# Index queries projected in three rounded passes, after the index keys, in a one-layer streaming encoder step

## The chip, the cores and the metric

The kernel runs as one program on one core of a Trainium2 chip. The metric is device time in microseconds (us). Before the change three runs gave a median of 1030.94 us (1030.78 to 1036.11).

The core has five engines that run side by side and meet only at semaphores: PE (matrix multiplies and transposes, with results in PSUM, the accumulator memory), DVE (vector work), ACT (activations and copies), POOL (a slower vector engine that also issues some transfers) and SP (which here only issues DMA transfers). On-chip data lie in SBUF.

## The reference, cut to what matters

One layer of an encoder is computed for 512 prompt tokens and 32 sample tokens, 1024 features each: a normalised input `h`, one wide projection of it, window attention, sparse attention, a merge, then a mixture of experts and an embedding gate. The change is in the part that picks keys for the sparse attention:

```python
qa, ka, va, qb, kb, vb, iq, ik, iw, ga, gb = jnp.split(jnp.dot(h, w_in), IN_SPLITS, axis=-1)
...
dots = jnp.einsum('bqhd,bsd->bqhs', iq, ik) * IDX_SCALE
score = jnp.einsum('bqh,bqhs->bqs', iw * IDX_HEAD_SCALE, jax.nn.relu(dots))
_, sel = lax.top_k(score, topk)
```

`iq` are the index queries (8 heads of 64, so 512 columns of `w_in`), `ik` the index keys (64 columns), `iw` 8 weights. A separate small table `rel_bias` gives a bias by the distance of query and key.

## The kernel before, in words

Every engine has one list of instructions, in the order in which the code writes them; nothing reorders them. Two tables only number the PSUM buffers: `WIDE` (three slots of two banks) and `NARROW` (two slots of one bank). Each says, for a use, which slot it gets and which earlier use must have been read out first, and by which engine.

The 544 tokens are in five tiles (four of 128, one of 32). The 1024 features are eight planes of 128. The steps of the front, in PE's order:

1. Transposes of the five normalised tiles (L900). DVE reads them out and multiplies by the gain (L1856): that is `hT`, the input with features on the partitions.
2. The bias table: one product of 32 buckets by 384 distances (L905). DVE reads it out, changes it in two small steps (L1875 to L1878) and signals `tabp_ready`. SP waits for this signal before it issues the write of the table, 128 times repeated, to memory outside the core (`toeplitz`, 3 MB). POOL waits for the same signal (L745) before it starts on its own list.
3. The index queries: four groups `m` of 128 columns, in each eight planes by two halves of 272 tokens, in plain f32 (`project`, L881).
4. The index keys and weights `ikw`: for each token tile eight products with 72 columns, in plain f32 (L888).
5. The keys turned: the prompt's (L920), then the cached ones and the sample's (L925, L926).
6. `dots`: 24 products for the prompt and 2 groups for the sample, each over a high and a low part of the keys (L940, L936). ACT applies the relu (L1522), DVE adds up the scores (L1914, L1917) and later picks the best eight at a time (L1933, L1937).
7. Keys and values of the sparse branch (`kvb`), then of the window branch (`kva`), in three passes each (L952), with their transposes; then the queries `qb` and `qa`, in three passes (L980). Then attention begins (L1014).

Three passes means this: a value `v` is split into a rounded high part (type fp32r, made by ACT, L1490) and the rounded remainder (made by DVE or POOL, L743, L758). Then high by high, high by low and low by high are added up in PSUM. `hT_f` and `hT_lo` are the two parts of `hT` for all 544 tokens. For step 7 they are made while steps 3 and 4 run.

After each index query group ACT stores a rounded high part (L1503) and DVE the remainder (L1886); after the turned keys the same two (L1507, L1900).

`slab[0]` is the SBUF place of the index query weights, and then of the `qb` weights; `slab_ikw` that of the key weights, and then of the `kva` weights. SP issues the `qb` load once the last index query group is in PSUM, and the `kva` load once the prompt's keys are turned. Both come behind the `toeplitz` write in SP's list and in its DMA queue.

On ACT the list after the last relu is: wait for the `kva` weights, make their high part (the `high` helper, L1490), then read out the five `kvb` tiles (L1532), each of which frees a `NARROW` slot.

Of the kernel before, what the change touches and what calls it, by code (L numbers as in the profile page):

```python
# [23 lines left out]
F32 = mybir.dt.float32  # L24
# [8 lines left out]
P = 128  # L33
# [43 lines left out]
CONSTS = 6  # L77
# [44 lines left out]
def ring(uses, slots):  # L122
# [16 lines left out]
    [(('xT', t), 'dve') for t in range(TILES)] + [(('iq', m), 'dve') for m in range(4)]  # L139
    + [(('ikT', s), 'dve') for s in 'ps']  # L140
# [4 lines left out]
    [('table', 'dve')] + [(('ikw', t), 'dve') for t in range(TILES)]  # L145
# [79 lines left out]
def _program(nc, A, ctx):  # L225
# [26 lines left out]
    def sem(name):  # L252
        return ctx.enter_context(nc.semaphore(name))
# [25 lines left out]
    for lo, hi in ((0, 16), (16, 24), (24, 32), (32.5, 40.5), (40.5, 48.5), (48.5, 56.5), (68.5, 73), (80, 97), (97.25, 114.25)):  # L279
        twin(arena, "front", int(lo * 256), int(hi * 256))  # L280
# [34 lines left out]
    hT_lo = at(114.25, [KD, NT])  # L315
    score = hb[:, 0:3 * (PAST + NS)].rearrange("p (b n) -> p b n", b=3)
# [157 lines left out]
    consts_in, gains_in = sem("consts_in"), sem("gains_in")  # L474
# [64 lines left out]
    def _(sp):  # L539
# [7 lines left out]
        for n, g in enumerate(['g_attn', 'g_ffn', 'g_ple']):  # L547
            load(gains[:, n, :], A[g][0].rearrange("(p c) -> p c", c=KD), gains_in)
# [19 lines left out]
        load(sink_in[:, :], A['attn_sink'].to_broadcast([P, HEADS]), consts_in)  # L568

# [146 lines left out]
    def _(pool):  # L716
# [28 lines left out]
        pool.wait_ge(tabp_ready, 1)  # L745
# [3 lines left out]
        pool.wait_ge(sw_high, 1)  # L749
# [10 lines left out]
        pool.wait_ge(sw_high, 2)  # L760
# [8 lines left out]
        query_weights_low(3, slab[0], qb)  # L769
# [13 lines left out]
        query_weights_low(7, slab[1], qx)  # L783
# [84 lines left out]
    def _(pe):  # L868
# [26 lines left out]
        for t in range(TILES):  # L895
# [7 lines left out]
        pe.wait_ge(table_in, 32)  # L903
        open_slot(NARROW, 'table', narrow_out)
        pe.matmul(ps[0:16, 6, 0:DIST], relb[0:BUCKETS, :], onehot[0:BUCKETS, :], start=True, stop=True)\  # L905
            .then_inc(narrow_full, 1)

        pe.wait_ge(slab_in['iq'], 16)
        pe.wait_ge(wide_out['dve'], WIDE[('xT', 4)].out)
        for m in range(4):  # L910
            slot = open_slot(WIDE, ('iq', m), wide_out)
            project(slot, lambda c: slab[0][:, c, m * P:(m + 1) * P], P, None, 0).then_inc(wide_full, 1)
        pe.wait_ge(slab_in['ikw'], 16)
        for t in range(TILES):
            slot = open_slot(NARROW, ('ikw', t), narrow_out)
            by_token(ps[:, 6 + slot, :], slab_ikw, IKW, t).then_inc(narrow_full, 1)
        w = wide(open_slot(WIDE, ('ikT', 'p'), wide_out))
# [3 lines left out]
        mm.then_inc(wide_full, 1)  # L921
        w = wide(open_slot(WIDE, ('ikT', 's'), wide_out))
# [23 lines left out]
        for br, s, c_k, kv_n in (('b', slab_kvb, cb_k, kv_b), ('a', slab_kva, None, kv_a)):  # L946
            pe.wait_ge(sw_split, 'ba'.index(br) + 1)
# [24 lines left out]
        for n, (q, s, dst) in enumerate((('qb', slab[0], qb), ('qa', slab[1], qx))):  # L972
            for m in range(4):
                w = wide(open_slot(WIDE, (q, m), wide_out))
                pe.wait_ge(sw_split, 3 + 4 * n + m)
# [494 lines left out]
    def _(act):  # L1470
# [10 lines left out]
        for t in range(TILES):  # L1481
            act.wait_ge(x_in[t], 16)
            r = ROWS[t]
            act.activation(xf[0:r, t, :], x_nat[0:r, t, :], ACT.Square, accum_out=nrm[0:r, t:t + 1]).then_inc(squares, 1)
# [14 lines left out]
        for m in range(4):  # L1499
# [5 lines left out]
        for i, (part, lo, cols) in enumerate((('p', 0, NP), ('s', NP, PAST + NS))):  # L1505
            w = wide(close(WIDE, ('ikT', part), wide_full))
            act.activation(rounded(ik_hi[:, lo:lo + cols], "front"), w[:, 0:cols], ACT.Copy).then_inc(ik_high, 1)  # L1507

# [311 lines left out]
    def _(dve):  # L1820
# [48 lines left out]
        dve.wait_ge(gains_in, 48)  # L1869
# [3 lines left out]
        dve.wait_ge(consts_ready, 1)  # L1873
        close(NARROW, 'table', narrow_full)
        dve.tensor_copy(tab[0:16, :], ps[0:16, 6, 0:DIST]).then_inc(narrow_out['dve'], 1)  # L1875
        dve.wait_ge(narrow_out['dve'], NARROW['table'].out)
        link(dve.tensor_tensor(nrm[0:16, 31:32], tab[0:16, 0:1], nrm[0:16, 30:31], ALU.mult))
        dve.tensor_scalar(tab[0:16, :], tab[0:16, :], nrm[0:16, 31:32], -1.0, ALU.subtract, ALU.mult).then_inc(tabp_ready, 1)  # L1878
        dve.memset(msk, 0.0)

        for m in range(4):
# [8 lines left out]
        for t in range(TILES):  # L1890
            r = ROWS[t]
            slot = close(NARROW, ('ikw', t), narrow_full)
            src = ps[0:r, 6 + slot, :]
            dve.tensor_copy(ik_n[0:r, t, :].rearrange("p (a n) -> p a n", a=2),
                            src[:, 0:HD].unsqueeze(1).to_broadcast([r, 2, HD]))
            dve.tensor_scalar(iw_n[0:r, t, :], src[:, HD:IKW], IW_SCALE, None, ALU.mult).then_inc(narrow_out['dve'], 1)
        for i, (part, lo, cols) in enumerate((('p', 0, NP), ('s', NP, PAST + NS))):
# [3 lines left out]
                              rounded(ik_hi[:, lo:lo + cols], "front").bitcast(F32), ALU.subtract).then_inc(wide_out['dve'], 1)  # L1901

# [537 lines left out]
```

## Time and profile before

| what | value |
|---|---|
| three runs | 1030.94 us median (1030.78 to 1036.11) |
| the profiled execution, its own time | 1036.8 us |
| its span, first to last instruction | 1035.0 us |
| TensorE clock granted over the span (mean) | 0.967 of full speed |
| PE busy | 925.9 us (89% of the span) |
| DVE, ACT, POOL busy | 378.2, 256.5, 132.4 us |
| chain that ended last: PE, DMA, DVE, ACT | 63%, 29%, 4%, 2% |

A time in the trace is counted from the first instruction. A group of the profile names engine, source line, output and input, and how often it runs. A plain f32 matmul appears as two records, so 64 of them read x128. The front described above is the stretch from 0 to 162 us; attention, merge and routing follow, and then the expert weights are streamed.

### The profile page before, as it was taken

The numbers are of one execution on the slowest core, as the hardware profiler recorded it, in microseconds if no ns is written. First come the engines' busy times: TensorE is split into PE (matmuls) and PEld (weight loads), VectorE is DVE, ScalarE is ACT, GpSimd is POOL, SyncE is SP. The second block draws the span as 40 slices with busy tenths as digits, with TensorE's granted clock in tenths as the row PEclk, the third lists the DMA queues.
The fourth block names the chain that finished last, engine by engine and source line by source line (L and its number), as shares of the span: only waits on it lengthen the run. The fifth ranks groups of instructions, "written<-read, shape, count | busy, mean of one in ns | idle before, by whom it ended". The sixth has DMA issues, their size and how long they took to land.

```text
span 1035.0 us, 14155 instructions
## 1 busy us (share of the span) xinstructions
PE 925.9 (89%) x5699; PEld 591.2 (57%) x5702; DVE 378.2 (37%) x974; ACT 256.5 (25%) x523; POOL 132.4 (13%) x136
## 2 busy tenths in 40 slices
PE   7989999999999999998999977877887888887996
PEld 7869995456999998994333322322322222234775
DVE  4179996764233436453111101101101011102796
ACT  6244326764323233221000000000000000001542
POOL 2403701113030000001111110011010110000000
PEclk9999998999999999997999999999999899999998
DMA  9850602002834316366999999999999999996601
GB/s 265 118 152 2 203 1 62 1 2 68 263 105 120 78 46 244 128 236 239 427 427 425 427 428 428 424 428 425 429 426 426 427 426 425 427 428 264 254 22 66
DMA packets 60132, 263.72 MB, mean 255 GB/s; under 512 B 11054, under 2 KB 36030, under 8 KB 46224
## 3 DMA queue, kind: packets, MB, share of 16 engines
q1 hardware_dynamic: 54160, 250.99, 63.0%
q0 software_dynamic: 5296, 9.79, 2.6%
q10 hardware_dynamic: 624, 2.23, 0.6%
q8 instruction: 36, 0.59, 0.2%
q14 instruction: 16, 0.13, 0.0%
HBM read 253.99 MB, written 16.85 MB: 262 GB/s over the span
## 4 chain that ended last, share of the span: by engine, by line
PE 63%; DMA 29%; DVE 4%; ACT 2%; issue 1%; SPq 1%; DVEq 0%; ACTq 0%
DMA arena<-in_w_up 25%; PE ps L1111 13%; PE ps L1278 12%; PE ps L980 5%; PE ps L1143 4%; PE ps L1426 4%; PE ps L1303 3%; PE ps L881 3%; PE ps L952 3%; DMA arena<-in_w_ple 2%; PE ps L1044 2%; PE ps L1014 2%; PE ps L1065 2%; PE ps L1399 1%; PE ps L1172 1%
## 5 line engine op out<-in xcount | busy, mean ns | idle before, releaser
L1278 PE MATMUL ps<-arena,hT 128*64 128x512 f32 x960 | 234.5, 641 | 39.4 <-DMA arena<-in_w_up 39.2
L1278 PEld LDWEIGHTS ps<-arena,hT 128*64 128x64 f32 x960 | 71.6, 141 | 199.3 <-issue 149.4
L2211 DVE TENSOR_TENSOR xf<-xf,ps 128x256 f32<-128x256 f32 x32 | 13.5, 421 | 401.6 <-ACT xf L1699 379.1
L1111 PE MATMUL ps<-arena_merge,arena_merge 128*128 128x256 f32 x624 | 99.7, 287 | 0.0
L1303 PE MATMUL ps<-arena,xf 128*64 128x512 f32 x336 | 76.7, 598 | 12.8 <-DVE xf L2214 12.8
L1111 PEld LDWEIGHTS ps<-arena_merge,arena_merge 128*128 128x128 f32 x624 | 87.4, 188 | 0.0
L836 POOL DMA_INDIRECT expert_rows<-xf,arena x32 | 32.2, 1007 | 425.6 <-ACT xf L1703 399.8
L1111 PE MATMUL ps<-xf_merge,arena_merge 128*128 128x256 f32 x480 | 82.0, 288 | 0.0
L1699 ACT ACTIVATE xf<-ps 128x256 f32<-128x256 f32 x30 | 11.6, 385 | 259.1 <-PE ps L1278 259.1
L1111 PEld LDWEIGHTS ps<-xf_merge,arena_merge 128*128 128x128 f32 x480 | 69.3, 188 | 0.0
L1703 ACT ACTIVATE xf<-ps 128x512 f32<-128x512 f32 x30 | 17.9, 598 | 159.8 <-PE ps L1303 159.8
L1303 PEld LDWEIGHTS ps<-arena,xf 128*64 128x64 f32 x336 | 24.3, 136 | 50.8 <-issue 43.0
L1143 PE MATMUL ps<-arena_merge,arena_merge 128*128 128x256 f32 x304 | 49.0, 286 | 1.2 <-DVE arena_merge L2045 1.0
L1303 PE MATMUL ps<-hT,xf 128*64 128x512 f32 x176 | 40.2, 598 | 6.6 <-DVE xf L2214 5.2
L1426 PE MATMUL ps<-arena_gate,hT_gate 128*128 128x512 f32 x192 | 44.4, 391 | 1.1 <-ACT arena L1741 0.6
L1143 PEld LDWEIGHTS ps<-arena_merge,arena_merge 128*128 128x128 f32 x304 | 42.9, 191 | 2.5 <-DVE arena_merge L2045 2.0
L980 PE MATMUL ps<-xf_merge,arena_front 128*128 128x272 f32 x256 | 42.9, 289 | 0.0
L2045 DVE TENSOR_TENSOR arena_merge<-arena,arena_merge 128x256 fp32r<-128x256 f32 (+2 forms) x34 | 39.9, 1228 | 5.1 <-ACT arena_merge L1490 5.0
L1490 ACT ACTIVATE arena_merge<-arena 128x256 fp32r<-128x256 f32 (+3 forms) x43 | 37.1, 919 | 16.2 <-DMA arena<-in_w_branch_a 7.2
L1426 PEld LDWEIGHTS ps<-arena_gate,hT_gate 128*128 128x128 f32 x192 | 35.8, 188 | 9.1 <-ACT arena L1741 1.0
L980 PEld LDWEIGHTS ps<-xf_merge,arena_front 128*128 128x128 f32 x256 | 36.2, 189 | 0.0
L1559 ACT ACTIVATE hT<-ps 128x256 f32<-128x256 f32 (+3 forms) x64 | 25.0, 394 | 21.9 <-PE ps L1044 21.2
(309 smaller groups left out, 1311.1 us busy)
## 6 DMA issues: line engine op xcount, KB each, us to landing
arena<-in_w_gate SPq DMA_DIRECT2D x30, 2048.0 KB, 29.4
arena<-in_w_up SPq DMA_DIRECT2D x30, 2048.0 KB, 37.0
arena<-in_w_down SPq DMA_DIRECT2D x11, 2048.0 KB, 36.4
hT<-in_w_down SPq DMA_DIRECT2D x11, 2048.0 KB, 36.5
arena<-in_w_down SPq DMA_DIRECT2D x20, 1024.0 KB, 32.2
arena<-in_w_in SPq DMA_DIRECT2D x10, 1024.0 KB, 6.2
arena<-in_w_in SPq DMA_DIRECT2D x3, 2048.0 KB, 10.5
arena<-in_w_gate SPq DMA_DIRECT2D x8, 512.0 KB, 9.0
```

Source lines behind the costliest of these rows:

```text
L836: pool.indirect_dma_start(ys, bass.IndirectOffsetOnAxis(ap=of, axis=0), src, None, bounds_check=row_bound, oob_is_err=False).then_inc(s, 16)
L881: mm = pe.matmul(w[:, a * 512:a * 512 + HALF], lhs(c), hT[:, c, a * HALF:(a + 1) * HALF], start=c == 0, stop=c == KD - 1)
L952: mm = pe.matmul(ps[0:ROWS[t], 6 + slot, 0:256], rounded(st[:, c, tok(t)]), rounded(mv[:, c, :], "front"), start=c == 0 and k == 0, stop=c ...
L980: mm = pe.matmul(w[:, a * 512:a * 512 + HALF], rounded(st, "front"), rounded(mv[:, c, a * HALF:(a + 1) * HALF]), start=c == 0 and k == 0, ...
L1111: mm = pe.matmul(w[:, 2 * lo_t:lo_t + hi_t], rounded(st[:, c, cols]), rounded(mv[:, c, lo_t:hi_t]), start=c == 0 and k == 0, stop=c == pla ...
L1143: mm = pe.matmul(w[:, q * QW:(q + 1) * QW], rounded(st[t // 2][:, t % 2, m, :]), rounded(mv[:, m, :]), start=m == 0 and k == 0, stop=m == ...
L1278: mm = pe.matmul(ps[g * BLK:(g + 1) * BLK, 2 + s, :], xsT[:, c, col:col + BLK], expert_columns(k, slice(0, 2), c, g), start=c == 0, stop=c ...
L1303: mm = pe.matmul(ps[g * BLK:(g + 1) * BLK, 6 + s, :], hidT[s][:, c % 2, c // 2 * BLK:(c // 2 + 1) * BLK], dn_at(k, c)[:, g * 512:(g + 1) * ...
L1426: mm = pe.matmul(w[:, cols], rounded(st[:, c, :], "gate"), rounded(mv[:, c, cols], "gate"), start=c == 0 and k == 0, stop=c == KD - 1 and ...
L1490: return act.activation(rounded(dst, stage), src, ACT.Copy)
L1559: act.activation(pT_sb[k2][:, j % 2, 0:tiles, j // 2 % 2, :], ps[:, 4 + u % 2, 0:tiles * P].rearrange("p (k n) -> p k n", n=P), ACT.Copy)\
L2045: return dve.tensor_tensor(rounded(v, stage), v, rounded(hi, stage).bitcast(F32), ALU.subtract)
```

## The change

`ikw` moves ahead of the index queries, and the table product behind the first index query group. The index queries are computed in three passes, as the later projections are: `hT_f` and `hT_lo` are used, and the weights are split into `iq_hi` (ACT, four groups) and a remainder in place (DVE for groups 0 and 1, POOL for 2 and 3). The turned keys are put between the groups: prompt's keys after group 0 and the table, cached and sample keys after group 1. POOL no longer waits for the table before it makes `hT_lo`. SP loads the key weights ahead of the query weights, and two of the three gain vectors with the constants.

```diff
-    [('table', 'dve')] + [(('ikw', t), 'dve') for t in range(TILES)]
+    [(('ikw', t), 'dve') for t in range(TILES)] + [('table', 'dve')]
@@ SP
+        load_gain(0, x_in[4])
+        load(slab_ikw, w_in[:, :, C_IK:C_IK + IKW], slab_in['ikw'])
+        load(slab[0], w_in[:, :, C_IQ:C_IQ + 512], slab_in['iq'])
         load(onehot[0:BUCKETS, :], A['bucket_of_distance'], table_in)
         load(relb[0:BUCKETS, :], A['rel_bias'], table_in)
-        load(slab[0], w_in[:, :, C_IQ:C_IQ + 512], slab_in['iq'])
-        load(slab_ikw, w_in[:, :, C_IK:C_IK + IKW], slab_in['ikw'])
@@ POOL
-        pool.wait_ge(tabp_ready, 1)
         for c in range(KD):
             pool.wait_ge(f_high, c + 1)
             low_of(hT_lo[:, c, :], hT[:, c, 0:NT], hT_f[:, c, :]).then_inc(f_split, 1)
+        for m in (2, 3):
+            pool.wait_ge(sw_high, m + 1)
+            low_of(slab[0][:, :, m * P:(m + 1) * P], slab[0][:, :, m * P:(m + 1) * P], iq_hi[m], "front").then_inc(sw_split, 1)
@@ PE
-        def project(slot, lhs, n_lhs, s_in, col):
-            w = wide(slot)
-            for c in range(KD):
-                for a in range(2):
-                    mm = pe.matmul(w[:, a * 512:a * 512 + HALF], lhs(c), hT[:, c, a * HALF:(a + 1) * HALF],
-                                   start=c == 0, stop=c == KD - 1)
-            return mm
+        def index_queries(m):
+            w = wide(open_slot(WIDE, ('iq', m), wide_out))
+            pe.wait_ge(sw_high, m + 1)
+            for k in range(3):
+                if k == 2:
+                    pe.wait_ge(*((iq_split, m + 1) if m < 2 else (sw_split, m - 1)))
+                for c in range(KD):
+                    if m == 0 and k < 2:
+                        pe.wait_ge((f_high, f_split)[k], c + 1)
+                    st = slab[0][:, c, m * P:(m + 1) * P] if k == 2 else iq_hi[m][:, c, :]
+                    mv = hT_lo if k == 1 else hT_f
+                    for a in range(2):
+                        mm = pe.matmul(w[:, a * 512:a * 512 + HALF], rounded(st, "front"),
+                                       rounded(mv[:, c, a * HALF:(a + 1) * HALF]),
+                                       start=c == 0 and k == 0, stop=c == KD - 1 and k == 2)
+            mm.then_inc(wide_full, 1)
@@ ACT
+        act.wait_ge(slab_in['iq'], 16)
+        for m in range(4):
+            high(iq_hi[m], slab[0][:, :, m * P:(m + 1) * P], "front").then_inc(sw_high, 1)
         act.wait_ge(slab_in['kvb'], 16)
         high(kv_hi['b'], slab_kvb, "front").then_inc(sw_high, 1)
@@ DVE
+        for m in range(2):
+            dve.wait_ge(sw_high, m + 1)
+            lo = slab[0][:, :, m * P:(m + 1) * P]
+            dve.tensor_tensor(rounded(lo, "front"), lo, rounded(iq_hi[m], "front").bitcast(F32), ALU.subtract).then_inc(iq_split, 1)
```

PE's list between the transposes of the input and the first `dots` product, before (`arena` is the SBUF area of the weights, `x_nat` here holds the index keys):

```order
L900 MATMUL ps<-ident,xf 128x32 x8
L905 MATMUL ps<-arena 16x384
L881 MATMUL ps<-hT,arena 128x272 x64
L888 MATMUL ps<-arena,hT 128x72 x32
L888 MATMUL ps<-arena,hT 32x72 x8
L920 MATMUL ps<-ident,x_nat 128x128 x4
L925 MATMUL ps<-ident,x_nat 128x128 x4
L926 MATMUL ps<-ident,x_nat 128x32
L940 MATMUL ps<-arena_front_83,arena_front_85 128x256
```

The same stretch after the change (`xf_merge_68` is `hT_f`, `arena_merge_77` is `hT_lo`; L919 is the three-pass product, L886 the keys, L927 the table, L932, L938 and L939 the turned keys); of the third and fourth group, which read like the second, only the third's first row is shown:

```order
L898 MATMUL ps<-ident,xf 128x32 x8
L886 MATMUL ps<-arena,hT 128x72 x32
L886 MATMUL ps<-arena,hT 32x72 x8
L919 MATMUL ps<-xf_merge_68,arena_front_82 128x272 x16
L919 MATMUL ps<-arena_merge_77,arena_front_82 128x272 x16
L919 MATMUL ps<-xf_merge_68,arena_front_78 128x272 x16
L927 MATMUL ps<-arena 16x384
L932 MATMUL ps<-ident,x_nat 128x128 x4
L919 MATMUL ps<-xf_merge_68,arena_front_82 128x272 x16
L919 MATMUL ps<-arena_merge_77,arena_front_82 128x272 x16
L919 MATMUL ps<-xf_merge_68,arena_front_78 128x272 x16
L938 MATMUL ps<-ident,x_nat 128x128 x4
```

The 64 plain products become 192 rounded ones; the keys come first, and their transposes no longer stand last. The last thing ahead of the `dots` is now an index query group.

DVE's list from the last readout of the transposed input on, before:

```order
L1856 TENSOR_TENSOR hT<-ps,gains 128x8x32
L1875 COPY arena<-ps 16x384
L1877 TENSOR_TENSOR nrm<-arena,nrm 16x1
L1878 TENSOR_SCALAR arena<-arena,nrm 16x384
L1879 MEMSET arena 128x912
```

And after (the five pairs of L1903 and L1905 read out the keys; the first two pairs' rows are enough here):

```order
L1882 TENSOR_TENSOR hT<-ps,gains 128x8x32
L1903 COPY x_nat<-ps 128x128
L1905 TENSOR_SCALAR x_nat<-ps 128x8
...
L1905 TENSOR_SCALAR x_nat<-ps 32x8
L1909 TENSOR_TENSOR arena_front_78<-arena,arena_front_82 128x8x128 x2
L1916 TENSOR_TENSOR arena_front_85<-ps,arena_front_85 64x544 x2
L1929 COPY arena<-ps 16x384
L1931 TENSOR_TENSOR nrm<-arena,nrm 16x1
L1932 TENSOR_SCALAR arena<-arena,nrm 16x384
```

The table's last step, behind which SP's `toeplitz` write waits, moved behind the keys' readout, two weight remainders and the first index query group.

## Rows read from the trace of the kernel before

**Rows 1.** Chain of waits, 15 to 65 us: start us, length us, what.
```profile
19.93 0.74 PE ps L905 x2
20.68 29.53 PE ps L881 x128
50.20 8.23 PE ps L888 x80
...
58.95 0.64 PE ps L920 x4
...
61.73 0.52 PE ps L940 x2
```

**Rows 2.** Timeline of PE: start us, length us, work (the last turned keys).
```profile
59.95 0.24 PE L926 MATMUL ps<-ident,x_nat 32*128 32x32 f32 x1
```

**Rows 3.** Chain of waits, 75 to 165 us.
```profile
79.63 14.31 PE ps L952 x120
...
111.99 48.51 PE ps L980 x384
...
161.15 0.63 ACT arena L1549
```

**Rows 4.** Timeline of DVE: start us, length us, work [idle before <-releaser].
```profile
21.54 0.41 DVE L1878 TENSOR_SCALAR arena<-arena,nrm 16x384 f32<-16x384 f32 x1
...
51.59 1.46 DVE L1886 TENSOR_TENSOR arena_front<-ps,arena_front 64x544 fp32r<-64x544 f32 x2 [5.88 <-ACT arena_front L1503]
...
58.67 0.14 DVE L1896 TENSOR_SCALAR x_nat<-ps 32x8 f32<-32x8 f32 x1
...
160.44 0.67 DVE L1963 TENSOR_SCALAR arena<-sink_in 32x2 f32<-32x2 f32 x4
161.84 0.06 DVE L1966 MEMSET ps<- 128x4 f32 x1 [0.73 <-ACT arena L1549]
```

**Rows 5.** Timeline of ACT.
```profile
20.56 4.49 ACT L1490 ACTIVATE xf_merge<-hT 128x544 fp32r<-128x544 f32 x8 [3.56 <-DVE hT L1856]
24.96 1.89 ACT L1490 ACTIVATE arena_front<-arena 128x2048 fp32r<-128x2048 f32 x1
...
80.21 1.91 ACT L1490 ACTIVATE arena_front<-arena 128x2048 fp32r<-128x2048 f32 x1
82.72 0.39 ACT L1532 ACTIVATE x_nat<-ps 128x256 f32<-128x256 f32 x1 [0.59 <-PE ps L952]
```

**Rows 6.** Timeline of POOL.
```profile
22.03 10.42 POOL L743 TENSOR_TENSOR arena_merge<-hT,xf_merge 128x544 fp32r<-128x544 f32 x8 [19.13 <-DVE arena L1878]
32.41 4.53 POOL L743 TENSOR_TENSOR arena_front<-arena,arena_front 128x2048 fp32r<-128x2048 f32 x1
```

**Rows 7.** Groups by line and form, DVE, whole span: count, busy us, mean ns.
```profile
L2045 DVE TENSOR_TENSOR arena_merge<-arena,arena_merge 128x1024 fp32r<-128x1024 f32 x8 | 12.1, 1512 | 0.0
```

**Rows 8.** Timeline of SP's issues.
```profile
24.90 0.43 SPq L541 DMA_DIRECT2D sink_in<-in_attn_sink  x1
25.37 0.68 SPq L541 DMA_DIRECT2D toeplitz<-arena  x1
...
50.24 9.91 SPq L541 DMA_DIRECT2D arena<-in_w_in  x2
```

**Rows 9.** DMA issues, 25.3 to 25.5, 50.2 to 50.5 and 59.3 to 60 us: KB, us to landing.
```profile
toeplitz<-arena SPq DMA_DIRECT2D x1, 3072.0 KB, 33.7
...
arena<-in_w_in SPq DMA_DIRECT2D x1, 2048.0 KB, 14.4
...
arena<-in_w_in SPq DMA_DIRECT2D x1, 1024.0 KB, 7.7
```

**Rows 10.** Stretches: length, busy us of the engines, clock, DMA share, GB/s.
```profile
54.00:56.00 2.00, 2.00 (x20) 2.00 (x20) 0.49 (x4) 0.00 (x0) 0.00 (x0) 1.00 0.91 104
60.00:62.00 2.00, 0.46 (x4) 0.35 (x4) 1.65 (x5) 0.84 (x2) 0.68 (x2) 1.00 1.05 401
62.00:66.00 4.00, 3.94 (x19) 3.71 (x19) 3.58 (x10) 2.87 (x8) 0.00 (x0) 0.59 0.96 333
```

More of the change, by code:

```diff
@@ L315, in _program @@
     hT_lo = at(114.25, [KD, NT])
+    iq_hi = [at(kb, [KD, P]) for kb in (40.5, 44.5, 52.75, 56.75)]
     score = hb[:, 0:3 * (PAST + NS)].rearrange("p (b n) -> p b n", b=3)
@@ L901, in _ @@
             mm.then_inc(wide_full, 1)
[L903 to L908, printed above, removed]
+        pe.wait_ge(slab_in['ikw'], 16)
         pe.wait_ge(wide_out['dve'], WIDE[('xT', 4)].out)
[L910 to L913, printed above, removed]
         for t in range(TILES):
@@ L916, in _ @@
             by_token(ps[:, 6 + slot, :], slab_ikw, IKW, t).then_inc(narrow_full, 1)
+        def index_queries(m):
[14 more added lines that the diff above has]
+            mm.then_inc(wide_full, 1)
+        index_queries(0)
+        pe.wait_ge(table_in, 32)
+        slot = open_slot(NARROW, 'table', narrow_out)
+        pe.matmul(ps[0:16, 6 + slot, 0:DIST], relb[0:BUCKETS, :], onehot[0:BUCKETS, :], start=True, stop=True)\
+            .then_inc(narrow_full, 1)
         w = wide(open_slot(WIDE, ('ikT', 'p'), wide_out))
@@ L946, in _ @@
         for br, s, c_k, kv_n in (('b', slab_kvb, cb_k, kv_b), ('a', slab_kva, None, kv_a)):
-            pe.wait_ge(sw_split, 'ba'.index(br) + 1)
+            pe.wait_ge(sw_split, 'ba'.index(br) + 3)
             for t in range(TILES):
@@ L1481, in _ @@
         for t in range(TILES):
-            act.wait_ge(x_in[t], 16)
+            act.wait_ge(x_in[t], 16 if t < 4 else 32)
             r = ROWS[t]
@@ L1504, in _, with index_keys @@
             ins.then_inc(q_high, 1)
-        for i, (part, lo, cols) in enumerate((('p', 0, NP), ('s', NP, PAST + NS))):
+        def index_keys(part, lo, cols):
             w = wide(close(WIDE, ('ikT', part), wide_full))
             act.activation(rounded(ik_hi[:, lo:lo + cols], "front"), w[:, 0:cols], ACT.Copy).then_inc(ik_high, 1)
+        index_queries(0)
+        index_keys('p', 0, NP)
+        index_queries(1)
+        index_keys('s', NP, PAST + NS)
+        index_queries(2)
+        index_queries(3)
         def query_weights_high(s, dst):
@@ L1868, in _, with index_queries @@
         rstd(P, 3, rstd_ready, 2)
-        dve.wait_ge(gains_in, 48)
+        dve.wait_ge(x_in[4], 32)
         for t in range(TILES):
             turned(wide(close(WIDE, ('xT', t), wide_full)), ROWS[t], t, 0).then_inc(wide_out['dve'], 1)
[L1873 to L1881, printed above, removed]
+        for t in range(TILES):
+            r = ROWS[t]
+            slot = close(NARROW, ('ikw', t), narrow_full)
+            src = ps[0:r, 6 + slot, :]
+            dve.tensor_copy(ik_n[0:r, t, :].rearrange("p (a n) -> p a n", a=2),
+                            src[:, 0:HD].unsqueeze(1).to_broadcast([r, 2, HD]))
+            dve.tensor_scalar(iw_n[0:r, t, :], src[:, HD:IKW], IW_SCALE, None, ALU.mult).then_inc(narrow_out['dve'], 1)
+        for m in range(2):
+            dve.wait_ge(sw_high, m + 1)
+            lo = slab[0][:, :, m * P:(m + 1) * P]
+            dve.tensor_tensor(rounded(lo, "front"), lo, rounded(iq_hi[m], "front").bitcast(F32), ALU.subtract).then_inc(iq_split, 1)
+        def index_queries(m):
             w = wide(close(WIDE, ('iq', m), wide_full))
@@ L1888, in _, with index_keys @@
             ins.then_inc(wide_out['dve'], 1)
[L1890 to L1897, printed above, removed]
+        def index_keys(i, part, lo, cols):
             w = wide(close(WIDE, ('ikT', part), wide_full))
@@ L1901, in _ @@
                               rounded(ik_hi[:, lo:lo + cols], "front").bitcast(F32), ALU.subtract).then_inc(wide_out['dve'], 1)
+        index_queries(0)
+        dve.wait_ge(consts_ready, 1)
+        slot = close(NARROW, 'table', narrow_full)
+        dve.tensor_copy(tab[0:16, :], ps[0:16, 6 + slot, 0:DIST]).then_inc(narrow_out['dve'], 1)
+        dve.wait_ge(narrow_out['dve'], NARROW['table'].out)
+        link(dve.tensor_tensor(nrm[0:16, 31:32], tab[0:16, 0:1], nrm[0:16, 30:31], ALU.mult))
+        dve.tensor_scalar(tab[0:16, :], tab[0:16, :], nrm[0:16, 31:32], -1.0, ALU.subtract, ALU.mult).then_inc(tabp_ready, 1)
+        index_keys(0, 'p', 0, NP)
+        index_queries(1)
+        index_keys(1, 's', NP, PAST + NS)
+        dve.memset(msk, 0.0)
+        index_queries(2)
+        index_queries(3)
         dve.wait_ge(narrow_out['dve'], NARROW_DONE['dve'])
```

33 lines of the change are left out of this document (19 added, 14 removed).

## The prediction

> **What bounds the kernel now.** I read the chain of waits first. From 20.7 to 160.5 us it is nearly all PE: the index queries take 29.53 us, the keys 8.23 us, turned keys follow, and the `dots` start at 61.73 us [rows 1]; later `kvb` (120 records in 14.31 us) and the two query projections (384 matmuls in 48.51 us) run packed [rows 3]. ACT's last readout ends at 161.78 us, and attention starts behind it. Then I read DVE's timeline at the same end: its selection and bias work is over at 160.44 + 0.67 = 161.11 us, and it then waits 0.73 us for ACT [rows 4]. So two chains run side by side from the `dots` to attention: PE's (the longer) and DVE's, 0.7 us shorter. Both start with the first `dots`. A gain ahead of the `dots` goes through only if both keep it. Behind 162 us nothing is changed, and every later load waits for progress of PE, so what attention gains in its start the end gains too.
>
> **The index queries.** Removed: 64 plain f32 matmuls, 29.53 us, 461 ns each [rows 1]. Added: 4 groups of 48 rounded matmuls of the same 272 columns. The later query projections are the same operation on the same `hT_f` and `hT_lo`: 48.51 / 384 = 126.3 ns each [rows 3]. 48 take 6.06 us, four groups 24.25 us: 5.28 us less. I take this row, since form, operands and weight changes are alike. The bounds are 120 ns (`kvb`'s 14.31 / 120 = 119 ns, at 256 columns) and 130 ns, so 23.0 to 25.0 us.
>
> The Trainium skill, "TensorE: Matmul & The Clock Gate", section "Back-to-back issue gap", gives N / 2.4 + 2.5 ns from one matmul to the next, 116 ns for 272 columns. By that the groups would be 2.0 us shorter. The trace's 126.3 ns disagrees and decides.
>
> **PE's list from 20.68 us.** The keys still wait for the last readout of `hT`. The table's 0.74 us had stood ahead of that wait, under DVE's readout; now it stands on the path.
> - keys: 20.68 + 8.23 = 28.91
> - group 0: 34.97; table: 35.71; prompt's keys (0.64): 36.35
> - group 1: 42.41; cached and sample keys (59.59 to 60.19, 0.60 [rows 1, 2], with the handover 0.7): 43.1
> - groups 2 and 3: 49.2 and 55.3.
>
> The `dots` wait until group 3 is stored. Before, the last group was in PSUM at 50.21 and DVE had stored it at 51.59 + 1.46 = 53.05 [rows 1, 4], 2.84 us. So the `dots` start at 55.3 + 2.84 + 0.05 = 58.2 us, against 61.73: 3.5 us earlier. Of the 5.28 us saved, 0.7 goes to the table and 1.3 to a longer last handover (2.9 us without PE work instead of 1.54), and the wait for the keys' readout gives 0.4 back.
>
> **What must be ready in time.** Each is hidden if earlier than PE's need.
> - High weights: ACT ends `hT_f` at 25.05 [rows 5], then four pieces of 128x1024, half of the 1.89 us for 128x2048 each, 26.0 to 29.0. Group 0 needs the first at 28.9. The query weights have landed by then (DMA traffic ahead of it is unchanged). Slack 2.9 us.
> - `hT_lo`: POOL needs 10.42 us for eight planes [rows 6] and now starts behind the first `hT_f` plane, at 21.3, so it ends at 31.7. The second pass of group 0 runs from 30.9 and needs the last plane at 32.7. Slack 1.0 us.
> - Remainder of group 0: DVE is free at 28.91 + 0.38 (its last key readout ended 0.38 us behind PE [rows 1, 4]) = 29.3 and takes 1.5 us [rows 7]: 30.8, needed at 32.9. Groups 2 and 3 on POOL: half of 4.53 us each [rows 6], so 34.0 and 36.2, needed at 47. `kvb`'s remainder ends at 40.8, needed at 76.
>
> DVE's two remainders (29.3 to 32.3) and POOL's last planes (to 31.7) run side by side, each with two inputs from SBUF, and no row of this front shows such a pair. Were both at half speed, `hT_lo` would end near 34 and PE would lose 1.3 us (rival 4). The Trainium skill, "GPSIMD Engine Reference", section "Key points", says that POOL contends with DVE instructions that read two SBUF inputs; it gives no size for it.
>
> **The table and what queues behind it.** This is the term that decides. DVE finished the table at 21.54 + 0.41 = 21.95, 1.28 us behind its matmul [rows 1, 4]. Now its copy stands behind group 0's storing: 34.97 + 2.84 = 37.81, and 1.17 us on 38.98. SP, which had been busy until 25.33 with small loads [rows 8], is idle by then and issues `toeplitz` at 39.05 instead of 25.37. It took 33.7 us to land [rows 9], at 59.07, at a steady 104 GB/s with the DMA engines 91% busy [rows 10]. `qb` was issued at 50.24 and landed 14.4 us later, at 64.64; `kva` was issued at 50.24 + 9.91 - 0.54 = 59.6 and landed at 67.3, 8.2 us behind `toeplitz` [rows 8, 9]. Until `toeplitz` ended the rate did not rise (104 GB/s at 54 to 56 us, with `qb` issued; 401 at 60 to 62 [rows 10]), so the two loads stood in a queue behind it. Afterwards `toeplitz` lands at 39.05 + 33.7 = 72.75, `qb` and `kva` (issued at 55.3 and 56) behind it, `kva` at 81.0. `qb` is wanted only near 95.
>
> Who waits for `kva`? ACT, at once behind the last relu: 80.21 before [rows 5], 76.7 now. It sits until 81.0 (4.3 us), makes the high part (1.91), and only then reads out `kvb` tile 0 (0.39): PE may start tile 2 at 83.4. PE starts `kvb` at 79.63 - 3.5 = 76.1 and has tiles 0 and 1 (2.86 us each) done at 81.8. So PE stands for 1.6 us where it stood for none. The bounds: `toeplitz` streams at once, since nothing is ahead of it now, and `kva` lands at 79.3: no stall. The loads go through one after another in their own issue-to-landing times, 72.75 + 14.4 + 7.7 = 94.8: 15.4 us of stall. I take 81.0, since the same three transfers did that in the trace. `kva`'s remainder (4.6 us on POOL, to 87.5) is in time for 94.
>
> **Nothing else.** `msk`'s memset, the key stores of POOL and the gain loads have idle engines around them.
>
> **The sum.** DVE's chain starts 3.5 us earlier and ends at 157.6. PE's chain gains 3.5 - 1.6 = 1.9 and ACT's last readout ends at 159.9: still the later one. The profiled execution would take 1036.8 - 1.9 = 1034.9 us. That one lay 5.9 us above the median of the runs, 1030.94, and the difference carries over: 1029.0 us.
>
> **Rivals.**
> 1. *`kva` is in time* (its lower bound), or the matmuls come nearer to 120 ns: the gain is 3.5 to 4.5 us, 1026.9 us. For it: in the trace `toeplitz` had other loads ahead of it. Against: the three transfers filled the queue. DVE's chain, 0.7 us shorter and started by the same `dots`, does not stand in the way.
> 2. *The queue holds ACT for long.* From a landing at 82.9 on, nothing is left of the gain (81.0 + 1.9); each us beyond is lost one to one, and above 88.1 the kernel is over 0.5% slower. At the far bound, 94.8, the loss is 15.4 - 3.5 = 11.9 us, 1042.8 us. For it: POOL's key stores now fall into the `toeplitz` write. Against: they are small, and the queue ran at 401 GB/s as soon as `toeplitz` was through.
> 3. *The clock.* After the 1.54 us without PE work around 61 us the granted clock was 0.59 on the mean from 62 to 66 us [rows 10]: of these 4 us 3.3 us were at the lower level, 1.2 GHz. It cost little, since ACT and DVE set the pace of the `dots`. Now PE stands for 2.9 us ahead of the `dots` and 1.6 us in `kvb`. If `kvb` gets such a stretch, half of it is lost, 1.6 us on PE's chain: no change, 1030.7 us.
> 4. *PE waits in group 0 for POOL's planes*: 1.3 us of the 1.9 are gone, 1030.3 us. Against: slack 1.0 us at POOL's measured pace.
>
> **How the numbers follow.** A change of under 0.5% (5.2 us) can't be told from none by measurement. Forecast 50%; rival 1, 20%; rivals 3 and 4, 20%; rival 2 beyond the zero point, 10%, of which half above 0.5%. All of the first three lie within 0.5%, but part of rival 1 together with a luckier median of the runs may pass 5.2 us. So faster 0.07, same 0.87, slower 0.06. The range runs from 1026.0 (rival 1 with 120 ns) to 1033.0 (2 us beyond no change, the near half of rival 2).
>
> **What would show it.** The first `dots` at 58.2 us; 24.2 us for 192 matmuls without gaps in group 0; `toeplitz` issued at 39.05; `kva` landing near 81; ACT idle for about 4 us on a DMA ahead of its `kva` high part; a PE gap of 1 to 2 us in `kvb`, released by ACT's readout; attention starting near 160.1. I am wrong if PE has no gap in `kvb` (then rival 1), if it is over 3.5 us (rival 2), or if the front of PE's list waits for weights or for POOL.

## The result and the profile after

| | before | after |
|---|---|---|
| median of 8 runs each | 1035.87 us (1030.78 to 1037.47) | 1040.25 us (1036.55 to 1044.47) |
| profiled execution, its own time | 1036.8 us | 1039.61 us |
| its span | 1035.0 us | 1037.9 us |
| clock granted over the span | 0.967 | 0.963 |

After / before is 1.0059, with a 95% interval of 1.0035 to 1.0082: 0.6% slower (the two medians alone stand 0.4% apart). 1029.0 us was forecast, at most 1033.0, and slower had a chance of 0.06. The eight runs of the kernel before are the three on which the forecast stood and five later ones, and those lay higher (1035.20 to 1037.47 us).

The chain of waits of the kernel after (start us, length us, what), where that of before is [rows 1, 3]:

```profile
19.68 14.05 PE ps L886 x80
33.73 7.02 PE ps L919 x48
...
42.08 6.01 PE ps L919 x48
...
48.70 12.21 PE ps L919 x96
...
60.93 0.61 ACT arena_front L1521
61.54 25.32 DMA arena<-in_w_in
...
86.89 1.91 ACT arena_front L1505
88.80 0.28 ACT x_nat L1558
```

Two lines catch the eye. The keys (L886) take 14.05 us where the same 80 records took 8.23 [rows 1]. And the chain passes through a weight load for 25.32 us: the `kva` weights.

Why the keys are slow stands in the stretches of the kernel after (length, busy us of PE, PEld, DVE, ACT and POOL with counts, clock, DMA share, GB/s; a clock of 1.00 is 2.4 GHz, 0.50 is 1.2 GHz):

```profile
18.00:20.00 2.00, 0.44 (x5) 0.35 (x5) 1.54 (x3) 0.43 (x1) 0.00 (x0) 1.00 0.87 257
20.00:22.00 2.00, 2.00 (x19) 2.00 (x19) 0.30 (x2) 2.00 (x5) 1.69 (x2) 0.94 1.10 275
22.00:24.00 2.00, 2.00 (x11) 2.00 (x11) 0.06 (x1) 2.00 (x5) 2.00 (x2) 0.50 0.81 87
...
32.00:34.00 2.00, 2.00 (x16) 1.80 (x15) 0.30 (x4) 0.00 (x0) 2.00 (x2) 0.50 0.00 0
34.00:36.00 2.00, 2.00 (x12) 2.00 (x12) 2.00 (x3) 0.00 (x0) 2.00 (x2) 0.64 0.00 0
```

PE is mostly idle from 18 to 20 us, then fully busy; at 21.8 us the clock falls to 0.50, and it comes back only at 35.4, when the wide products of group 0 have run for 1.7 us. The count of records tells the same: 19 in the 2 us that are nearly all at full clock, 11 at half. What stood in the gap before was the table's product; and in the traced execution of the kernel before, the transposes ahead of it ran at 1.2 GHz until 18.4 us and so lasted until 19.93, where here they ran at 2.4 GHz and ended near 18.1. PE's timeline of the kernel after shows the gap in brackets, and a second one in `kvb` (L967):

```profile
19.68 1.53 PE L886 MATMUL ps<-arena,hT 128*128 128x72 f32 x12 [1.56 <-DVE hT L1882]
...
89.12 0.50 PE L967 MATMUL ps<-arena_front,xf_merge 128*128 128x256 f32 x2 [1.53 <-ACT x_nat L1558]
```

The second gap was forecast, with its cause. SP's issues, and ACT's high part of `kva`, in the timelines of the kernel after:

```profile
44.83 0.68 SPq L542 DMA_DIRECT2D toeplitz<-arena  x1
60.93 10.66 SPq L542 DMA_DIRECT2D arena<-in_w_in  x2
```
```profile
86.89 1.91 ACT L1505 ACTIVATE arena_front<-arena 128x2048 fp32r<-128x2048 f32 x1 [4.51 <-DMA arena<-in_w_in]
```

The DMA issues of this kernel (KB, us from issue to landing) answer to [rows 9]:

```profile
toeplitz<-arena SPq DMA_DIRECT2D x1, 3072.0 KB, 32.6
...
arena<-in_w_in SPq DMA_DIRECT2D x1, 2048.0 KB, 22.4
...
arena<-in_w_in SPq DMA_DIRECT2D x1, 1024.0 KB, 25.3
```

`toeplitz` is issued 19.5 us later than before [rows 8], and the loads behind it land late; ACT sits 4.5 us and then reads out `kvb`'s first tile.

Two more lines matter, though their cost is hidden here. They are DVE's remainders of the query weights for groups 0 and 1 (in the view of that line: ns of the shortest, the median and the longest, and when the first and the last began), and POOL's timeline at that time:

```profile
L1909 DVE TENSOR_TENSOR arena_front<-arena,arena_front x2: 2393/4002/5611, 34.1 to 36.4; 128x1024 fp32r<-128x1024 f32 x2
```
```profile
20.31 10.43 POOL L748 TENSOR_TENSOR arena_merge<-hT,xf_merge 128x544 fp32r<-128x544 f32 x8 [17.39 <-ACT xf_merge L1505]
30.71 10.19 POOL L748 TENSOR_TENSOR arena_front<-arena,arena_front 128x1024 fp32r<-128x1024 f32 x3
```

Two instructions that were priced at 1.5 us each took 2.39 and 5.61 us. The second ended at 41.98, 1.08 us behind POOL's last remainder, that of `kvb`, which took 5.57 us and ended at 40.90.

Attention starts at 165.69 us, in DVE's timeline of the kernel after, against 161.84 [rows 4]:

```profile
165.69 0.06 DVE L2003 MEMSET ps<- 128x4 f32 x1 [2.37 <-ACT arena L1575]
```

The 3.85 us split into 2.07 at the start of the `dots` (63.80 against 61.73) and 1.78 behind it, in `kvb`. The span grew by 2.9 us, the median by 4.4. A single execution can differ that much in the later stages: from the start of attention to the end, where nothing was changed, the ten traced executions of this document took between 867.4 and 873.6 us (873.2 before, 872.2 after). In the two shortest, e2 and e3 below, the clock stayed at 1.00 from 162 to 300 us, where it was 0.96 on the mean before and after. So the start of attention, and not the total of one execution, is what the traces are compared by below.

One thing doesn't fit a simple rule on pauses. PE stood for 2.90 us ahead of the `dots` and 1.53 us in `kvb`, and the clock fell behind neither; it is at 1.00 from 52 to 110 us:

```profile
62.00:66.00 4.00, 2.10 (x13) 1.70 (x13) 3.50 (x10) 1.50 (x6) 0.00 (x0) 1.00 0.89 103
```

In the kernel before, 1.54 us were enough at the same place [rows 10].

### The profile page after: what moved, and what is told of

Same layout as the page of the kernel before. It is cut to its first block, busy times and chain, and to the rows that moved or that the text cites. A ratio compares the mean times of both kernels' runs of the same rounds, so it can differ in the third digit from the quotient of the medians.

```text
span 1037.9 us, 14298 instructions
## 1 busy us (share of the span) xinstructions
PE 928.5 (89%) x5766; PEld 593.4 (57%) x5766; DVE 386.0 (37%) x976; ACT 259.6 (25%) x527; POOL 138.0 (13%) x138
## 4 chain that ended last, share of the span: by engine, by line
PE 60%; DMA 31%; DVE 4%; ACT 2%; issue 1%; SPq 0%; DVEq 0%; ACTq 0%
DMA arena<-in_w_up 26%; PE ps L1126 13%; PE ps L1293 12%; PE ps L995 5%; PE ps L1158 4%; PE ps L1441 4%; PE ps L1318 3%; DMA arena<-in_w_in 2%; PE ps L919 2%; DMA arena<-in_w_ple 2%; PE ps L967 2%; PE ps L1059 2%; PE ps L1029 2%; PE ps L1080 2%; PE ps L886 1%
## 5 line engine op out<-in xcount | busy, mean ns | idle before, releaser
L1293 PE MATMUL ps<-arena,hT 128*64 128x512 f32 x960 | 238.8, 651 | 35.4 <-DMA arena<-in_w_up 35.2
L765 POOL TENSOR_TENSOR arena_front<-arena,arena_front 128x512 fp32r<-128x512 f32 (+1 forms) x17 | 24.7, 1491 | 60.2 <-ACT arena_front L1505 60.2
```

What stands on the lines that cost most here:

```text
L765: return pool.tensor_tensor(rounded(v, stage), v, rounded(hi, stage).bitcast(F32), ALU.subtract)
L1293: mm = pe.matmul(ps[g * BLK:(g + 1) * BLK, 2 + s, :], xsT[:, c, col:col + BLK], expert_columns(k, slice(0, 2), c, g), start=c == 0, stop=c ...
```

## The experiments

The theory after the first look: (A) PE's pause ahead of the keys brings the clock down, and the keys pay for it; (B) the late table delays `toeplitz` and `kva`, and costs `kvb` its gap; (C) DVE and POOL hold each other up. The rival to A is that the keys are slow for want of something else (weights, the load traffic); to B, that the gap comes from ACT's longer list. All ratios are against runs of the kernel before on the same chip (medians 1035.87 us for e1 to e4, 1036.61 for e5 to e8). Each kernel has one trace.

### The pause filled, and the late write (A, B)

**e1_fill** puts work that nobody reads into PE's pause:

```diff
+        for _ in range(6):
+            pe.matmul(ps[:, 7, 0:P], ident[:, :], ident[:, :], start=True, stop=True)
         pe.wait_ge(slab_in['ikw'], 16)
```

> The changed kernel with six plain 128x128 matmuls of the identity put on PE between the transposes of the input and the keys, where PE stood idle from 18.1 to 19.7 us. Theory (the pause there brings the lower clock, and the keys' narrow products run through on it: 14.05 us instead of 8.23, and group 0 7.02 instead of 6.06): keys in about 8.3 us, group 0 in 6.1 if DVE's remainder is in time, the dots start near 57 to 59 us instead of 63.80, attention 5 to 6 us earlier less a longer stall in kvb, since the kva load shifts as much as the dots do. Rival (the keys are slow in first place because their load or DVE's readout holds them, not the clock): the keys still take about 14 us and nothing moves. Second thing to read: DVE's and POOL's remainders side by side took 3.97 and up to 3.4 us a piece; if that stands, group 0's third pass will wait 1 to 3 us for DVE, as DVE starts at 28 and is not done before 32.

Measured: median 1036.11 us (12 runs), ratio 1.0016 (0.9998 to 1.0034). The chain of waits of this kernel:

```profile
17.98 1.53 PE ps L902 x12
...
19.54 8.45 PE ps L886 x80
28.00 6.23 PE ps L921 x48
...
37.68 4.21 DVE nrm L1933
...
42.98 12.28 PE ps L921 x96
...
55.89 28.72 DMA arena<-in_w_in
```

A stands: 1.5 us of matmuls that nobody reads, and the keys take 8.45 us, with the clock at full from 20 to 34 us. The transposes ran at full clock here as in the kernel after, so what sets the two traces apart ahead of the keys is the filled pause. The `dots` start at 58.15, 5.65 us earlier. The median is 4.1 us below that of the kernel after, but attention starts only 0.7 us earlier (164.98), since the other two causes now came out. DVE's step on 16 numbers took 4.2 us, till POOL's long remainder was over, and held up PE's group 2 by 0.80 us (C); and as PE was earlier and `kva` was not, the gap in `kvb` grew, in PE's timeline of this kernel:

```profile
86.87 0.54 PE L969 MATMUL ps<-arena_front,xf_merge 128*128 128x256 f32 x2 [4.93 <-ACT x_nat L1560]
```

Behind this gap the clock was low once more (0.67 on the mean from 88 to 92 us), and 72 records of `kvb` took 10.22 us instead of 8.68.

**e2_late_table** puts the `toeplitz` write behind the `qb` and `kva` loads in SP's list:

```diff
-        sp.wait_ge(tabp_ready, 1)
-        load(toep_d, tab[0:16, :].unsqueeze(1).to_broadcast([16, P, DIST]), toep_moved)
...
+        sp.wait_ge(tabp_ready, 1)
+        load(toep_d, tab[0:16, :].unsqueeze(1).to_broadcast([16, P, DIST]), toep_moved)
```

> The changed kernel, but SP issues the toeplitz write behind the qb and kva loads instead of ahead of them. Theory (kva stands in the queue behind toeplitz, ACT waits 4.5 us for it and PE 1.8 us in kvb): kva lands by about 71, no wait of ACT on a DMA and no PE gap in kvb, attention starts 1.8 us earlier (163.9), with the dots still at 63.8; toeplitz lands near 105, before it is read. Rival (the gap comes from ACT's own work or from POOL): attention still starts at 165.7.

Measured: median 1039.9 us (12 runs), ratio 1.0027 (0.9998 to 1.0057). In the chain of waits of this kernel `kvb` runs without a gap, but the front ahead of it is slower still:

```profile
20.72 15.56 PE ps L885 x80
...
36.66 5.39 DVE arena_front L1908
...
85.40 14.36 PE ps L966 x120
```

B stands too: with `kva` ahead of the write nobody waits for a load, and from the `dots` to attention it takes 100.15 us where the kernel after took 101.89. But attention was expected at 163.9 and came at 167.65, as the `dots` came at 67.50 and not at 63.8: in this execution the clock fell already at 21.2 us, so that the keys took 15.56 us, and DVE's remainder, held by POOL, was waited for. PE's pause ahead of the keys was shorter here (0.98 us), since the transposes ran at 1.2 GHz until 17.8 us. Two of the twelve runs took 1027.5 and 1027.8 us. They have no trace; what they did differently stays open.

**e4_both** has both of these edits, e1's and e2's.

> e1 and e2 together: pause filled, toeplitz behind qb and kva. Theory: the two causes add up: dots at 57 to 59 us, no gap in kvb, attention at 158 to 160, 6 to 8 us below the changed kernel and 2 to 4 us below before. Rival (one cause hides the other): no better than the better of e1 and e2.

Measured: median 1034.07 us (12 runs), ratio 0.9982 (0.9962 to 1.0002). Keys 8.45 us, `dots` at 58.35, `kvb` without a wait for a load, attention at 158.88, 3.0 us ahead of before: the two causes add up, as expected. The ratio's interval just includes no change. e2 and e4 differ by the filled pause alone, and their medians by 5.8 us, so A shows in the times too. DVE's table step was again held, until 42.13; that no longer delayed a load, but still held up PE's group 2 by 0.79 us.

### The table first (A, B and what C costs)

**e3_table_first** brings the table's loads, product and readout back to where they were before the change; all else is the change's.

```diff
-    [(('ikw', t), 'dve') for t in range(TILES)] + [('table', 'dve')]
+    [('table', 'dve')] + [(('ikw', t), 'dve') for t in range(TILES)]
@@ PE, ahead of the keys
+        pe.wait_ge(table_in, 32)
+        slot = open_slot(NARROW, 'table', narrow_out)
+        pe.matmul(ps[0:16, 6 + slot, 0:DIST], relb[0:BUCKETS, :], onehot[0:BUCKETS, :], start=True, stop=True)\
+            .then_inc(narrow_full, 1)
```

> The changed kernel with the table (its loads, product and readout) back where it stood before, ahead of the keys; three-pass queries, keys first, and turned keys between the groups stay. Theory: toeplitz is issued near 25 us again, no wait in kvb; the table's 0.74 us fills half of PE's pause, so the clock may or may not fall. If it stays at the higher level the keys take 8.3 us and the dots start near 57 us, attention near 156 to 158, total 4 us below before; if it falls, dots at 63 and attention at 163. Rival (the three passes or the contention of DVE and POOL are what costs): dots not before 61 even with keys at 8.3 us.

Measured: median 1036.02 us (12 runs), ratio 1.0021 (1.0000 to 1.0041); the profiled execution took 1028.97. The chain of waits of this kernel:

```profile
21.80 13.01 POOL arena_merge L748 x8
...
34.86 2.53 PE ps L923 x18
```

PE's pause is 0.45 us (the transposes ran at 1.2 GHz until 17.1 us, which made it short), the clock stays full over the keys, `toeplitz` goes out at 26.59, and `kvb` has no gap; the `dots` start at 59.64 where 57 was expected, attention at 159.80 where 156 to 158 was. The median shows nothing of these 2 us against before: the low 1028.97 of the traced execution comes from behind the start of attention, and whether the clock also stayed full ahead of the keys in the others isn't known. Here PE is early and group 0 waits for POOL's eight planes until 34.81. Seven took 1.34 us each and one 3.72, the one beside DVE's two weight remainders, which took 1.20 us each. This is rival 4 of the prediction, and it is only seen once PE isn't slow itself.

**e5_pool_waits** is e1_fill, and POOL waits for the table before its long remainder:

```diff
+        pool.wait_ge(tabp_ready, 1)
         pool.wait_ge(sw_high, 5)
```

> The kernel of e1_fill with one more wait: POOL makes kvb's remainder (4.6 us in one instruction) only when DVE has finished the table. In e1_fill the table's middle step sat on DVE from 37.7 to 41.9 us, ending with POOL's instruction (41.87). Theory (a DVE instruction that takes two inputs from SBUF, or works on SBUF alone at double pace, and a POOL instruction exclude each other, and DVE waits for the whole POOL instruction): the table's steps take 0.6 us again, toeplitz is issued near 38.3 instead of 42.5, kva lands 4 us earlier, PE's gap in kvb falls from about 5.5 to about 1.5 us, and group 2 no longer waits for DVE (1.2 us). Attention 4 to 5 us earlier than in e1_fill. Rival (the step waits for something else, such as the semaphore of the first step): the step ends at 41.9 again and toeplitz stays at 42.5.

Measured: median 1035.11 us (10 runs), ratio 0.9984 (0.9970 to 0.9999). DVE's steps and POOL's remainder, in the timelines of this kernel:

```profile
38.78 0.15 DVE L1934 TENSOR_TENSOR nrm<-arena,nrm 16x1 f32<-16x1 f32 x1
```
```profile
39.45 4.59 POOL L748 TENSOR_TENSOR arena_front<-arena,arena_front 128x2048 fp32r<-128x2048 f32 x1 [1.08 <-DVE arena L1935]
```

The 4.20 us of e1 become 0.15: it was POOL. `toeplitz` goes out 3.0 us earlier (39.40) and the gap in `kvb` shrinks from 4.93 to 2.76 us. Attention starts at 162.84, 2.1 us ahead of e1 where 4 to 5 were expected: the front of this execution began 1.4 us later (keys at 20.91 against 19.54), and the gap, put at 1.5 us, was 2.76, since `toeplitz` went out 1.1 us later than expected.

### The two halves of the change apart

**e6_order_alone** keeps the change's order but computes the queries in plain f32 as before:

```diff
-            pe.wait_ge(sw_high, m + 1)
-            for k in range(3):
...
+            pe.wait_ge(slab_in['iq'], 16)
+            for c in range(KD):
+                for a in range(2):
+                    mm = pe.matmul(w[:, a * 512:a * 512 + HALF], slab[0][:, c, m * P:(m + 1) * P],
+                                   hT[:, c, a * HALF:(a + 1) * HALF], start=c == 0, stop=c == KD - 1)
```

> The order of the change without its passes: keys first, table behind group 0, turned keys between the groups, but index queries in plain f32 from hT, with no weight remainders. Theory (the order, by the pause ahead of the keys, costs the clock): keys again at 12 to 14 us on the lower clock when it falls in the pause; group 0 partly at the lower clock (8 to 10 us), then 7.4 us a group; dots near 69 us, toeplitz later than in the change, attention 5 or more us behind the change, total 1042 to 1046. Rival (rounded passes are what lowers the clock, or POOL's and DVE's remainders what slows the front): keys at 8.3 us, dots near 62, total as before.

Measured: median 1044.42 us (4 runs), ratio 1.0082 (1.0065 to 1.0098). The chain of waits and the stretch of the keys of this kernel:

```profile
20.03 14.12 PE ps L883 x80
34.15 8.32 PE ps L909 x32
...
51.74 14.88 PE ps L909 x64
```
```profile
20.00:34.00 14.00, 13.97 (x80) 13.75 (x80) 1.46 (x8) 6.20 (x9) 13.35 (x9) 0.57 0.45 103
```

The order alone costs all of it: the clock falls at 22.1 us and the keys take 14.12 us, with no three-pass product among the index queries. The `dots` start at 69.51 (69 was expected).

**e7_passes_alone** keeps the three passes but puts the order back (table, four groups, keys, turned keys):

```diff
-        index_queries(0)
...
+        for m in range(4):
+            index_queries(m)
+        pe.wait_ge(slab_in['ikw'], 16)
+        pe.wait_ge(wide_out['dve'], WIDE[('xT', 4)].out)
+        for t in range(TILES):
+            slot = open_slot(NARROW, ('ikw', t), narrow_out)
...
-        index_queries(1)
...
-        index_queries(2)
-        index_queries(3)
```

> The passes of the change without its order: table first, four query groups in three passes, then the keys and the turned keys, as before. Theory: no queue behind a late table and keys at 8.3 us on the higher clock, but group 0 must wait for POOL's planes (ready at 32 to 34 us), so the groups end near 52.5 us instead of 50.2 and the dots start at 64, some 2 us behind before; total 1035 to 1039. Rival (the passes alone give their 5.3 us): dots at 56.5.

Measured: median 1040.83 us (10 runs), ratio 1.0032 (1.0014 to 1.0050). PE's timeline of this kernel:

```profile
25.21 3.97 PE L919 MATMUL ps<-xf_merge,arena_front 128*128 128x272 f32 x16 [6.40 <-ACT arena_front L1504]
...
32.90 0.52 PE L919 MATMUL ps<-arena_merge,arena_front 128*128 128x272 f32 x2 [0.78 <-POOL arena_merge L748]
```

PE waits 6.4 us for ACT's first high part, which the expectation had left out, and then for POOL's last two planes; the clock falls at 22.5 us, within that wait, and comes back at 29.3. The `dots` start at 64.94 (64 was expected), and the median lies above the 1035 to 1039 us expected. So the keys did belong ahead of the queries: they are the work under which ACT and POOL prepare. The change's parts need each other, and the order needs the pause closed.

### A version that keeps the gain

**e8_dve_remainders** is e3_table_first, three filling matmuls behind the table, the eight planes of `hT_lo` made by DVE, two ahead of each readout of a key tile, and POOL's remainders behind DVE's last one:

```diff
-        for c in range(KD):
-            pool.wait_ge(f_high, c + 1)
-            low_of(hT_lo[:, c, :], hT[:, c, 0:NT], hT_f[:, c, :]).then_inc(f_split, 1)
+        pool.wait_ge(iq_split, 2)
@@ DVE, ahead of the readout of key tile t
+            for c in range(2 * t, 2 * t + 2) if t < 4 else ():
+                dve.wait_ge(f_high, c + 1)
+                dve.tensor_tensor(rounded(hT_lo[:, c, :]), hT[:, c, 0:NT], rounded(hT_f[:, c, :]).bitcast(F32), ALU.subtract)\
+                    .then_inc(f_split, 1)
```

> A version meant to beat both: table first (as e3), three plain fill products behind it, the eight remainders of hT on DVE (two ahead of each key readout) instead of POOL, and POOL's three remainders only behind DVE's. Theory (exclusion of DVE and POOL is what is left): DVE needs about 0.65 us a plane, nothing waits, keys from 19.7 to 28.0, groups without a gap, dots at 56.4, no gap in kvb, attention near 156.5: 5.3 us below before and 9 below the change; total 1029 to 1031. Rival (the pace of DVE's remainders is no better when POOL is idle, or the clock still falls): dots after 59.

Measured: median 1032.35 us (5 runs, 1031.61 to 1033.50), ratio 0.9960 (0.9947 to 0.9974). That is 0.4% faster than before; 1029 to 1031 us was expected. The kernel after was not run beside it, but its fastest run (1036.55) lies above the slowest here. The chain of waits, the two sides of the former conflict in DVE's and POOL's timelines, and the start of attention of this kernel:

```profile
21.12 8.22 PE ps L884 x80
29.34 6.20 PE ps L923 x48
...
35.97 6.01 PE ps L923 x48
...
42.60 12.21 PE ps L923 x96
...
57.70 0.81 PE ps L955 x2
...
75.89 14.35 PE ps L967 x120
```
```profile
29.66 2.34 DVE L1920 TENSOR_TENSOR arena_front<-arena,arena_front 128x1024 fp32r<-128x1024 f32 x2
...
158.12 0.06 DVE L2008 MEMSET ps<- 128x4 f32 x1 [0.60 <-ACT arena L1575]
```
```profile
32.08 9.30 POOL L748 TENSOR_TENSOR arena_front<-arena,arena_front 128x1024 fp32r<-128x1024 f32 x3 [29.18 <-DVE arena_front L1920]
```

The front from the keys on is what the prediction had drawn up: 8.22, 6.20, 6.01, 12.21 us without a wait. Attention starts at 158.12, 3.7 us ahead of before, and the median is 4.3 us lower. The `dots` were expected at 56.4; they came 1.3 us later, as the keys started 1.4 us later than expected (21.12: the transposes ran partly at 1.2 GHz and ended at 19.51, and the three filling matmuls then stood on the path).

## Why the prediction was wrong

- **The failed step: "keys: 20.68 + 8.23 = 28.91".** The term measured 14.05 us, 5.8 too few were counted, more than the whole expected saving of 3.5 us at the `dots`. I took 8.23 from a row at full clock and didn't ask what PE had done just before. I had seen that the table's product stood under DVE's readout, and I priced its move at the 0.74 us that it now takes on the path. What it did in its old place was to keep PE at work. The three executions traced with a pause of 0.98 to 1.56 us ahead of the keys (after, e2, e6) had the clock at half 0.5 to 2.1 us behind it; the five with 0.45 us or less there (e1, e3, e4, e5, e8) kept it at full through the keys. e1 changes nothing else and gives 5.6 us back.
- **Rival 3 (the clock)** was named, with [rows 10] as its reason, and put only at the `dots` and in `kvb`, where the clock of the kernel after stayed full. It was never laid against the pause that the change opens ahead of the keys. There the low level lasted 13.6 us, 11.9 of them under the keys, so a pause of 1.6 us cost 5.8.
- **The start of the keys** was put at 20.68; it was 19.68, since this execution's transposes ran at a higher clock. Before, they had been the end of the path. This gave 1.0 us back.
- **Group 0** took 7.02 us, not 6.06: the low clock reached 1.7 us into it. Group 1 took 6.01 us and groups 2 and 3 together 12.21, and without the low clock all four took 24.4 us (e8). **The size of the three-pass group was right**: 24.25 was forecast, at 126.3 ns a matmul. The runs, at 125 ns (6.01 us for 48), go with the row. By the formula of the Trainium skill, "TensorE: Matmul & The Clock Gate", section "Back-to-back issue gap", it would have been 2.0 us less, an estimate; but the same section says that this formula is for a matmul by itself and leaves out the weight loads, which the prediction didn't mention, and each matmul here has one.
- **The last handover** was put at 2.9 us and was 2.89 (60.91 to 63.80). The sum to the `dots`, 58.2, thus misses 63.80 by 5.8 (keys) + 1.0 (group 0) - 1.0 (start), and 0.2 or less elsewhere.
- **The queue term was right**, in mechanism and size. `toeplitz` landed 32.6 us behind its issue, `kva` at 86.9, 9.4 us behind `toeplitz` (forecast: 8.2); ACT sat 4.5 us (4.3); `kvb` lost 1.8 us (1.6). Being late by the same amount as PE, table and `kvb` kept their distance. e2 and e4 show the cause: with the write behind the loads the gap is gone.
- **Rival 4** (POOL's planes against DVE's remainders) was put at 1.3 us and "against: slack 1.0 us". In the kernel after it cost nothing, since PE was slower still. In e3 it decided. The mechanism is another than half speed for both: see below. The DVE remainders' price, 1.5 us from [rows 7], is 1.20 us where POOL doesn't hold them up (e3, e8).
- **The sum.** Attention was forecast at 160.1 and came at 165.69. Of the 5.6 us the `dots` make all. The forecast time stood 11.2 us below the median measured: 5.6 for this, 4.9 because before's median was 1035.87 and not the 1030.94 of its first three runs, and 0.7 in the later stages and scatter. The 4.9 us say nothing of the mechanism: two of the first three runs happened to be low ones, which is bad luck with a small sample.

Put together: of the 5.3 us that the three passes save, the change as written gets nothing, because the pause costs 5.8 us in the keys and 1.0 in group 0; and the late table takes 1.8 us more. At the start of attention it gets 3.0 us with the pause closed and `kva` in time (e4), and 3.7 us with DVE and POOL apart too (e8).

## What to carry to other kernels

An instruction under somebody else's wait is not free to move: ask what its engine does in the hole that it leaves, and, on PE, lay the granted clock over that place before a duration is taken from a row at full clock. Before moving the producer of a slow transfer, list what is queued behind the transfer and by when each of those is wanted. When one cause is taken away, look in the trace for the next one in line; here each of three held back what the others would have given. And look at the level of the clock ahead of a pause too: transposes at half clock end later and make the pause behind them shorter, so the pause need not be the same in every execution (1.56 us in the kernel after, 0.98 in e2). No kernel here was traced twice, so how often each happens isn't known.

## What the runs showed of the hardware

**The same narrow products ran on at either level of the clock.** PE is 100% busy from 22 to 34 us in the kernel after and stays at 1.2 GHz. The 80 records of the keys began at 2.4 GHz in every kernel; behind the pause the clock fell 2.1 us into them, and without it they stayed at 2.4 GHz to their end (8.22 to 8.45 us in e1, e3 to e5, e8). The stretch in e1, which holds the keys and most of group 0:

```profile
20.00:34.00 14.00, 14.00 (x126) 13.82 (x125) 6.14 (x12) 9.51 (x13) 13.83 (x9) 1.00 0.42 93
```

and in the kernel after:

```profile
20.00:34.00 14.00, 14.00 (x80) 13.67 (x80) 1.68 (x10) 9.64 (x13) 13.69 (x10) 0.56 0.40 92
```

The busy shares are the same. What divides the two is the 1.56 us ahead, idle in the one and filled in the other. Wide products came back sooner: in e7 group 0 (272 columns) began at 1.2 GHz at 25.21 us and had 2.4 GHz at 29.3, and in e1 `kvb` (256 columns) began again at 86.87, fell to 1.2 GHz at 87.2 and had 2.4 GHz back at 90.6.

**A pause didn't always bring the clock down.** Behind 1.54 us ahead of the `dots` it fell in the kernel before and in e7. With 2.90 us there it fell, within the pause or soon behind it, in e1 to e4, e6 and e8, but not in the kernel after and not in e5. With 1.53 us in `kvb` it stayed up in the kernel after, and with 2.76 us in e5 it fell. So the length of the pause alone doesn't decide, and nothing here shows what else does.

**DVE and POOL take turns by whole instructions**, where both read two inputs from SBUF. A DVE remainder of 128x1024 took 1.20 us alone (e8), and 5.61 in the kernel after, where it ended 1.08 us behind POOL's remainder of 128x2048; that one took 5.57 us, against 4.59 in e5. A DVE step on 16 numbers took 4.20 us (e1) or 0.15 (e5); POOL's plane took 3.72 instead of 1.34 (e3) beside two of DVE's, and 1.34 + 2 x 1.20 is 3.74. So each stands until the other's current instruction is through, however small its own work is. The Trainium skill, "GPSIMD Engine Reference", section "Key points", says that the two contend here; the runs agree, and add the size. Also, DVE made a plane of 128x544 in 0.72 us (e8) where POOL took 1.34.

**Not settled:** the two runs of e2 near 1027.5 us, and why some pauses leave the clock up. That the narrow products themselves keep the clock down was not tested apart: no run put wide ones in their place behind the same pause.
